# A projection chunk split around the transposes of the attention probabilities

## The reference

```python
h = rmsnorm(x, norm_g)
a_u, a_v, a_z, b_b, b_c, b_x, b_z, c_q, c_k, c_v, c_z, d_q, d_k, d_v, d_z = split(h @ w_in)
y_a = conformer_conv(a_u, a_v, ...) * silu(a_z)        # 31 taps, then layernorm
y_b = short_gated_conv(b_b, b_c, b_x, ...) * silu(b_z)  # 3 taps
y_c = window_gqa(rope(c_q), rope(c_k), c_v, sink) * silu(c_z)      # 4 heads of 64
y_d = neighborhood_attn(d_q, d_k, d_v, rpb) * silu(d_z)            # 4 heads of 64, learned bias
x = x + concat(y_a, y_b, y_c, y_d) @ w_out
```

## Time and profile before

| what | value |
|---|---|
| median of 3 runs | 2291.18 us (2290.15 to 2292.41) |
| the profiled execution | 2291.51 us |
| its span, first to last instruction | 2289.3 us |
| TensorE busy | 2085.9 us (91%) |
| VectorE busy | 1306.3 us (57%) |
| GpSimd busy | 1067.6 us (47%) |
| ScalarE busy | 756.3 us (33%) |

### The profile page before, as it was taken

One profiled execution on the slowest core, in us unless ns is written; L12 is line 12 of the kernel. 1 busy time (PEld: TensorE's weight loads), 2 busy tenths in 40 slices (PEclk: granted clock), 3 DMA queues, 4 the chain that ended last, 5 costly groups with the idle time before them and its releaser, 6 DMA issues.

```text
span 2289.3 us, 30906 instructions
## 1 busy us (share of the span) xinstructions
PE 2085.9 (91%) x9708; PEld 1728.9 (76%) x9708; DVE 1306.3 (57%) x2241; ACT 756.3 (33%) x1101; POOL 1067.6 (47%) x1301
## 2 busy tenths in 40 slices
PE   5988887998887899979999999978899899999997
PEld 4877666877665788868788888867787788888886
DVE  5377766378768655464545535465555445535445
ACT  3232332332332344443232232234444323232231
POOL 3333244334233343456656655634435465656653
PEclk9999898999897899989999999989989899999998
DMA  4111112212111121122222222211222222222221
GB/s 153 64 57 71 38 56 80 76 55 74 38 56 67 56 74 55 74 92 85 89 100 95 92 92 96 106 63 57 73 73 74 77 107 79 106 92 92 96 98 62
DMA packets 28052, 179.66 MB, mean 78 GB/s; under 512 B 4000, under 2 KB 4128, under 8 KB 7456
## 3 DMA queue, kind: packets, MB, share of 16 engines
q1 hardware_dynamic: 24192, 169.88, 20.7%
q10 hardware_dynamic: 3744, 8.34, 1.1%
HBM read 176.11 MB, written 2.10 MB: 78 GB/s over the span
## 4 chain that ended last, share of the span: by engine, by line
issue 48%; POOL 35%; PE 17%; DVE 0%; POOLq 0%; DVEq 0%; ACT 0%
POOL W_lo L422 35%; PE bank L436 16%; POOLq L417 0%; DVE X L1626 0%; PE bank L486 0%; PE bank L479 0%; POOLq L419 0%; POOL spare L413 0%; DVE TMP L1283 0%; DVE PR L1328 0%; DVE PRE L1325 0%; DVE X L1989 0%; DVE PR L1986 0%; DVEq L182 0%; POOLq L422 0%
## 5 line engine op out<-in xcount | busy, mean ns | idle before, releaser
L422 POOL TENSOR_TENSOR W_lo<-W_raw,W_hi 128x256 fp32r<-128x256 f32 x1280 | 1065.7, 868 | 1189.7 <-ACT W_hi L867 1189.6
L436 PE MATMUL bank<-H_hi,W_hi 128*128 128x512 f32 x1392 | 560.3, 402 | 20.2 <-POOL W_lo L422 17.4
L436 PE MATMUL bank<-H_lo,W_hi 128*128 128x512 f32 x1392 | 549.8, 395 | 0.0
L436 PE MATMUL bank<-H_hi,W_lo 128*128 128x512 f32 x1392 | 549.7, 395 | 0.0
L867 ACT ACTIVATE W_hi<-W_raw 128x2048 fp32r<-128x2048 f32 x161 | 307.4, 1910 | 395.3 <-PE bank L436 382.5
L436 PE MATMUL bank<-Y_hi,W_hi 128*128 128x512 f32 x836 | 338.3, 405 | 21.9 <-DVE Y_lo L1268 11.8
L436 PE MATMUL bank<-Y_lo,W_hi 128*128 128x512 f32 x836 | 335.5, 401 | 0.0
L436 PE MATMUL bank<-Y_hi,W_lo 128*128 128x512 f32 x836 | 335.1, 401 | 0.0
L436 PEld LDWEIGHTS bank<-H_hi,W_hi 128*128 128x128 f32 x1392 | 267.4, 192 | 82.3 <-issue 22.3
L436 PEld LDWEIGHTS bank<-H_hi,W_lo 128*128 128x128 f32 x1392 | 265.9, 191 | 57.6
L436 PEld LDWEIGHTS bank<-H_lo,W_hi 128*128 128x128 f32 x1392 | 267.1, 192 | 53.0
(11 more groups left out here) (265 smaller groups left out, 2753.2 us busy)
## 6 DMA issues: line engine op xcount, KB each, us to landing
W_raw<-in_stream SPq DMA_DIRECT2D x160, 1024.0 KB, 4.8
BT<-in_bias ACTq DMA_DIRECT2D x8, 448.0 KB, 3.6
X<-in_x ACTq DMA_DIRECT2D x4, 512.0 KB, 9.7
out<-X SPq DMA_DIRECT2D x8, 256.0 KB, 2.2
BT<-in_rope ACTq DMA_DIRECT2D x2, 512.0 KB, 3.5
MC<-in_causal ACTq DMA_DIRECT2D x2, 320.0 KB, 3.0
MS<-in_window ACTq DMA_DIRECT2D x1, 320.0 KB, 11.0
CS<-in_rope ACTq DMA_DIRECT2D x1, 256.0 KB, 2.5
```

Source lines behind the costliest of these rows:

```text
L422: ins = nc.gpsimd.tensor_tensor(W[1][:, s, part], W_raw[:, s, part], W[0][:, s, part].bitcast(F32), ALU.subtract)
L436: mm = pe.matmul(out, lhs[a], rhs[b], start=(not begun and k == 0 and a == 0 and b == 0), stop=(not more and k == n - 1 and a == 1), skip_ ...
```

## The change

In steps 0 to 13 the chunk is cut in two. Its first four contraction tiles (12 matmuls) go between the scores and the transposes, the other four stay behind the transposes. The accumulation in `G[c]` stays open in between. The waits for the weights and for the bank go with the first half, the signal that the chunk is done stays with the second. Steps 14 and 15 (`o00`, `o01`) are as before. Nothing is changed on the other engines.

```diff
+            def first_half(name):
+
+                n = B1_CHUNKS.index(name)
+                k, c = divmod(n, 2)
+                if c == 0:
+                    begin_unit(1, l, k)
+                free_bank(n)
+                three(pe, G[c][:, :], chunk_pairs(k % 2, c, H)[:KT // 2], more=True)
+
+            def second_half(name):
+
+                k, c = divmod(B1_CHUNKS.index(name), 2)
+                three(pe, G[c][:, :], chunk_pairs(k % 2, c, H)[KT // 2:], begun=True).then_inc(b1.done.sem, 1)
...
                 if i % STEPS < STEPS - 1:
                     scores(i + 1)
+                halved = i in FILL and FILL[i][0] != "o"
+                if halved:
+                    first_half(FILL[i])
                 transposes(i)
-                if i in FILL:
+                if halved:
+                    second_half(FILL[i])
+                elif i in FILL:
                     chunk(FILL[i])
```

## The result

The changed kernel takes 2300.01 us, median of 5 runs (2299.3 to 2303.18), against 2291.18 (2289.33 to 2292.52) for the kernel before on the same chip. The ratio is 1.0041, with a 95% interval of 1.0026 to 1.0055: slower, by 8.8 us. 2300.8 was predicted. Its profiled execution took 2299.67 us with a span of 2297.5.

The account below looks back on a forecast made before the run. TensorE was taken to set steps 0 to 4, VectorE with its ScalarE exchanges the rest. 2 x (4.6 + 0.2) = 9.6 us on the profiled 2291.51 gives 2301.1, less 0.3 for the median: 2300.8, range 2296.8 to 2304.8.

Parts of the forecast that it names:

- Half a chunk: The 12 matmuls put ahead of the transposes in steps 0 to 13 take 2.8 us.
- The switch of operands: Each cut step switches TensorE's operands once more, taken as 0.1 us, between nothing and 0.25.
- Step 0: The first half waits 0.2 us for GpSimd's W_lo; transposes move by 3.0 us, TensorE ends 0.3 late.
- Steps 1 and 3: The next scores newly wait 0.64 and 0.55 us for VectorE's row maxima; TensorE is 1.79 us late in total.
- The hand-over: At step 4 the transposes move by 1.79 + 2.8 = 4.6 us, and VectorE's whole second regime with them.
- Steps 5 to 13: Existing waits cover the half chunk, except step 12 at the lower clock, 0 to 0.7 us late, taken as 0.2.
- The waits for the probabilities: TensorE's 15 waits at block 1's transposes, 19.3 us in total; filling them with the half chunk buys nothing.
- The other layer repeats the pattern: Both layers lose alike, so the sum is 2 x (4.6 + 0.2) = 9.6 us.
- +0.2: Loss a layer behind step 4, taken for step 12's transposes running late at the lower clock.
- the prediction's own signs: Lateness stays 4.6 to 5 us to layer end; wrong if shrinks or grows over 0.5 us in steps 6 to 15.
- rival D: Steps 6 to 13: half chunks fill waits for probabilities, giving back up to 19.3 us; faster, 2281; chance 0.04.
- rival C: Steps 6, 8, 10, 12: half chunk at lower clock makes transposes late, at most 2.8 us a layer; 2303.2; chance 0.09.

Follow-up runs that it names:

- experiment two: The changed kernel with the chunk cut in step 4 only; 2295.43 us, ratio 1.0019.
- Experiment four: The changed kernel with two contraction tiles (6 matmuls) instead of four ahead of the transposes in steps 0 to 13; 2293.17 us, ratio 1.0009.
- experiment five: The changed kernel with VectorE's scaling of the next bias tile moved ahead of the split of the transposes in steps 1, 3 and 5; 2298.70 us.
- experiment one: The changed kernel with the chunk cut in steps 0 to 3 only; 2298.67 us, ratio 1.0030.
- Experiment three: The changed kernel with the chunk cut in steps 5 to 13 only; 2290.09 us, ratio 0.9994.
- experiment nine: The kernel before with two of the convolution's taps moved from step 4 into step 3 on VectorE; 2288.83 us, ratio 0.9985.
- experiment seven: The kernel before with bias tiles scaled early and, in step 4 alone, the transposes ahead of the scores; 2288.15 us, ratio 0.9987.

## Why the prediction was right

The time was 0.8 us off, and the steps up to step 4 stand nearly as summed.

- *Half a chunk, 2.8 us.* From 91.83 to 94.68 it took 2.85; in experiment two it moved the split of step 4 by 2.8.
- *The switch of operands, 0.1 a step.* Scores without a wait came 0.39 us later behind step 0, W_lo's 0.26 among it: 0.13, close to the 0.1 taken.
- *Step 0, 0.2 us for W_lo.* 0.26, and the transposes 3.19 later (3.0 summed).
- *Steps 1 and 3, new waits of 0.64 and 0.55.* 0.60 and 0.56, for VectorE's L1367 as named. Experiment four shows the margin, and experiment five, in which one of them goes and the other is halved, the chain.
- *Step 2, no wait.* None.
- *The hand-over, 4.6.* 4.69 us in both layers. Here the sum left out a way: I let step 4's transposes hang on TensorE's order alone. In after the probabilities of step 4 are there 1.7 us before the transposes start (132.55 against 134.30), because the half chunk stands in between; without it, as in experiment one, they are what the transposes wait for. The sum came out right only because the half chunk is longer than the 1.10 us that experiment one's transposes wait.
- *Steps 5 to 13, covered.* Experiment three shows it up to step 7 (0.04 us), and its time is no different. For steps 8 to 13 it shows next to no cost (0.2 us), but layer 2 of the changed kernel does lose there and in step 6, as told below.
- *The waits for the probabilities.* Filling them bought nothing, as the rows said: the wait at the transposes went from 19.3 to 0.5 us in after and to 1.4 in experiment three, and experiment three's time can't be told from that of before.

**What was missed.** "The other layer repeats the pattern" and "+0.2" a layer for the rest. Behind step 4 the layers lost +0.2 in neither: layer 1 came down from 4.6 to 3.5, layer 2 went up to 6.2. By the prediction's own signs this part is wrong in both layers: the distance was to stay at 4.6 to 5 us to the end of the layer, and it shrank by more than 1 us in one and grew by 1.5 in the other. It shrank in the five chunks behind step 7, and not, as rival D has it, because waits for probabilities were filled. The loss in layer 2 is rival C in small. In its step 6:

```profile
504.27 0.79 PE L436 MATMUL bank<-AK_hi,AQ_hi 64*128 64x512 f32 x1 [0.24 <-DVE SM L1367]
504.87 0.62 PE L436 MATMUL bank<-AK_lo,AQ_hi 64*128 64x512 f32 x1
...
511.07 1.03 PE L494 MATMUL bank<-ident,PR 128*128 128x128 f32 x8
...
512.22 1.09 ACT L891 ACTIVATE PT_hi<-bank 128x512 fp32r<-128x512 f32 x2 [0.41 <-PE bank L494]
```

The clock is at its lower level from 502.6 to 509.4, scores and most of the half chunk run at it, and ScalarE, for which VectorE's output had always been the last thing, waits 0.41 us for the transposes. The split of step 6 is 0.5 us later than in layer 1. Another 0.3 us follows at step 8 and 0.8 at step 14, which has no cut chunk: there the chunk starts at 664.1 and the clock is at its lower level until 669.9, while in before the chunk starts at 653.7 and the clock is back at 657.7. No term of the sum had that. The gain in layer 1 is the kernel before's own loss, told in the last section. How often an unprofiled execution takes which way isn't known, nor why the unchanged block 2 takes 3 us less in one profile than in the other. Over the twelve profiles what follows layer 2's last transposes has two lengths, 1624.8 to 1625.5 us in five (after among them) and 1627.2 to 1628.3 in seven (before among them). With some 3 us of such scatter, a median within 0.8 us of the sum is partly luck. The sign, and the 4.7 us a layer at step 4, are not.

## What to carry to other kernels

Idle time of the busiest engine is not a place to put work in, unless that engine ends the loop: before moving work ahead of an instruction, follow that instruction's result through the other engines, and write down the smallest margin on the way; here it was 2.06 us for a half chunk of 2.85. Look for the step at which another engine takes over, since here a lateness brought to that point was kept whole through the steps that the other engine sets (4 to 7), and so was a gain, such as that of two taps moved into a wait of 1.67 us on VectorE. Beyond those steps neither was safe: the same five chunks gave back or took 2 us in some layers and not in others, so an effect of a few us is read stretch by stretch from a common event, and not from the medians alone. And where a result has two ways to an instruction, price both: a sum with only one of them is right until an edit makes the other the later.

## What the runs showed that was not expected

The five chunks between the attended values of step 7 and the scores of step 8 run in two ways, in kernels in which not one of their instructions is changed. The sums of that stretch in the two layers of before, the two of after, and the two of experiment nine:

```profile
172.49:208.98 36.49, 34.24 (x193) 29.62 (x192) 25.78 (x38) 10.44 (x11) 14.48 (x19) 0.95 0.21 80
521.04:554.28 33.24, 32.71 (x193) 28.53 (x192) 24.86 (x36) 10.44 (x11) 14.48 (x19) 1.00 0.21 73
```

```profile
179.57:212.97 33.40, 33.40 (x192) 29.31 (x192) 24.70 (x35) 10.45 (x11) 14.05 (x19) 0.97 0.20 72
531.20:564.57 33.37, 33.37 (x192) 29.28 (x192) 24.70 (x35) 10.44 (x11) 14.03 (x19) 0.97 0.20 71
```

```profile
170.88:207.37 36.49, 34.24 (x193) 29.64 (x192) 25.78 (x38) 10.44 (x11) 14.48 (x19) 0.95 0.22 80
515.88:552.35 36.47, 34.23 (x193) 29.60 (x192) 25.75 (x38) 10.45 (x11) 14.48 (x19) 0.95 0.22 79
```

TensorE in before, layer 1 and then layer 2, ahead of the stretch and at its third chunk:

```profile
170.97 0.38 PE L436 MATMUL bank<-PT_hi,AV_hi 128*128 128x256 f32 x1 [2.77 <-DVE PT_lo L1268]
...
185.79 0.49 PE L436 MATMUL bank<-H_hi,W_hi 128*128 128x512 f32 x1 [2.25 <-POOL W_lo L422]
...
186.96 0.63 PE L436 MATMUL bank<-H_lo,W_hi 128*128 128x512 f32 x1
...
518.32 0.58 PE L436 MATMUL bank<-PT_hi,AV_hi 128*128 128x256 f32 x1 [2.79 <-DVE PT_lo L1268]
...
532.72 0.49 PE L436 MATMUL bank<-H_hi,W_hi 128*128 128x512 f32 x1 [0.53 <-POOL W_lo L422]
```

GpSimd's subtraction for that third chunk, and the sums of 4 us behind the wait, in layer 1 and in layer 2:

```profile
179.18 6.48 POOL L422 TENSOR_TENSOR W_lo<-W_raw,W_hi 128x256 fp32r<-128x256 f32 x8 [9.14 <-ACT W_hi L867]
526.54 6.05 POOL L422 TENSOR_TENSOR W_lo<-W_raw,W_hi 128x256 fp32r<-128x256 f32 x8 [9.14 <-ACT W_hi L867]
...
186.20:190.20 4.00, 4.00 (x12) 3.14 (x11) 3.12 (x5) 1.37 (x2) 0.00 (x0) 0.57 0.73 262
533.50:537.50 4.00, 4.00 (x19) 3.31 (x18) 3.79 (x6) 0.00 (x0) 0.00 (x0) 1.00 0.78 266
```

In layer 2 the clock is low already when the attended values of step 7 begin (0.58 us for the first matmul, 0.38 in layer 1), they take 1.2 us longer, and TensorE comes later to the third chunk's weights, for which it then waits 0.53 us. In layer 1 it comes early, waits 2.25 us, the clock drops right behind (0.57 over 4 us, matmuls of 0.63 us), and the stretch takes 3.25 us longer; 1.2 of it were won ahead, so 2.05 us are lost. Of these 0.4 are GpSimd's, which in both layers starts 8.2 us behind the first of the attended values but takes 6.48 us in place of 6.05, and 1.6 come behind the wait. Over the 24 layers of the twelve kernels the six with a wait of 2.24 or 2.25 us are the six that took 36.5 us, and the 18 others waited 0.53 us or less and took 33.2 to 34.2.

So a layer can get 2 us of a debt back, or lose 2 us of a gain, in code that nobody touched. Which of the two it is doesn't follow from being late or early: layer 2 of experiment one, 3.5 us late, is among the six, and layer 1 of experiment seven, 0.6 us early, is not. What goes with it in all 24 is the clock at step 7: in the six it is full when the attended values begin and while they run (1.5 us for the 12 matmuls), in the 18 it is low then or falls while they run (1.8 to 2.7 us). That it is the idle time at the third chunk which brings the clock down is what the order of the rows says in six of six; no run took the wait away by itself, and none shows why the clock is low at step 7 in one layer and full in another.
